# Moving the drains of woven matmul groups behind the next attention half step, in pieces

## Time and profile before

| what | us |
|---|---|
| median of 3 runs (1999.07 to 2000.43) | 1999.86 |
| the profiled execution's own time | 1998.55 |
| its span, first to last instruction | 1996.7 |
| PE busy in the span | 1897.4 (95%) |
| ACT busy | 906.2 (45%) |
| DVE busy | 778.3 (39%) |
| POOL busy | 661.8 (33%) |
| chain that ended last: share of PE | 82% |
| chain: DVE, ACT, issue | 9%, 6%, 3% |

### The profile page before, as it was taken

The page is one execution under the profiler, slowest core; times in us unless marked ns, Lnnn a source line. Parts: engine busy times, 40 slices in busy tenths (PEclk is TensorE's granted clock), DMA queues, the critical chain, the costliest instruction groups (busy, mean ns, idle before and its releaser), DMA issues.

```text
span 1996.7 us, 24926 instructions
## 1 busy us (share of the span) xinstructions
PE 1897.4 (95%) x9233; PEld 1546.8 (77%) x9239; DVE 778.3 (39%) x1346; ACT 906.2 (45%) x1775; POOL 661.8 (33%) x278
## 2 busy tenths in 40 slices
PE   8998999898999899989899999999999999999998
PEld 6887777676788777777676888888788878888886
DVE  3434655534543565544447672010350431111002
ACT  4555565543465556554353833233453353323222
POOL 2422333122242222322233444434103423444442
PEclk9998999999999899999999999999999999999999
DMA  4221212112322121211231222222102422222322
GB/s 153 85 74 43 74 65 74 53 43 106 116 85 66 51 72 66 74 53 43 104 138 65 95 95 95 86 94 89 60 1 75 142 78 97 95 95 95 99 101 85
DMA packets 44568, 163.74 MB, mean 82 GB/s; under 512 B 6192, under 2 KB 6448, under 8 KB 43824
## 3 DMA queue, kind: packets, MB, share of 16 engines
q1 hardware_dynamic: 42640, 148.65, 22.3%
q10 hardware_dynamic: 1824, 13.63, 1.8%
HBM read 155.97 MB, written 6.29 MB: 81 GB/s over the span
## 4 chain that ended last, share of the span: by engine, by line
PE 82%; DVE 9%; ACT 6%; issue 3%; DMA 0%; POOL 0%; DVEq 0%; ACTq 0%; POOLq 0%; SPq 0%
PE bank L644 12%; PE bank L646 12%; PE bank L645 12%; PE bank L647 10%; PE bank L649 10%; PE bank L648 10%; PE bank L771 2%; PE bank L788 2%; ACT q_dup L1013 2%; PE bank L749 1%; PE bank L747 1%; PE bank L750 1%; DVE y_tok L1398 1%; PE bank L735 1%; PE bank L708 1%
## 5 line engine op out<-in xcount | busy, mean ns | idle before, releaser
L627 POOL TENSOR_TENSOR w_hl<-w_raw,w_hl 128x1024 fp32r<-128x1024 f32 x274 | 661.6, 2419 | 1310.6 <-ACT w_hl L899 1310.0
L899 ACT ACTIVATE w_hl<-w_raw 128x1024 fp32r<-128x1024 f32 x274 | 287.6, 1058 | 343.7 <-DMA w_raw<-wstream 343.2
L644 PE MATMUL bank<-act_hl,w_hl 128*128 128x512 f32 x1056 | 428.4, 406 | 5.7 <-DVE q_low L1368 2.8
L646 PE MATMUL bank<-act_hl,w_hl 128*128 128x512 f32 x1056 | 415.4, 393 | 0.0
L645 PE MATMUL bank<-act_hl,w_hl 128*128 128x512 f32 x1056 | 415.1, 393 | 0.0
L647 PE MATMUL bank<-w_hl,act_hl 128*128 128x512 f32 x672 | 265.6, 395 | 6.1 <-DVE q_low L1368 4.0
L649 PE MATMUL bank<-w_hl,act_hl 128*128 128x512 f32 x672 | 262.3, 390 | 0.0
L648 PE MATMUL bank<-w_hl,act_hl 128*128 128x512 f32 x672 | 262.0, 390 | 0.0
L644 PEld LDWEIGHTS bank<-act_hl,w_hl 128*128 128x128 f32 x1056 | 201.1, 190 | 48.9 <-issue 5.7
L646 PEld LDWEIGHTS bank<-act_hl,w_hl 128*128 128x128 f32 x1056 | 200.2, 190 | 43.5
L645 PEld LDWEIGHTS bank<-act_hl,w_hl 128*128 128x128 f32 x1056 | 201.1, 190 | 40.3 <-issue 1.9
(11 more groups left out here) (232 smaller groups left out, 2839.7 us busy)
## 6 DMA issues: line engine op xcount, KB each, us to landing
w_raw<-wstream SPq DMA_DIRECT2D x274, 512.0 KB, 3.5
x_spill<-x_res ACTq DMA_DIRECT2D x2, 2048.0 KB, 7.0
x_res<-x_spill ACTq DMA_DIRECT2D x2, 2048.0 KB, 7.9
x_res<-x SPq DMA_DIRECT2D x4, 512.0 KB, 5.7
g_post<-post_gains ACTq DMA_DIRECT2D x4, 512.0 KB, 3.6
x_res<-x ACTq DMA_DIRECT2D x1, 2048.0 KB, 8.4
out<-x_res SPq DMA_DIRECT2D x4, 512.0 KB, 2.6
probs<-w_gates ACTq DMA_DIRECT2D x1, 1024.0 KB, 10.7
```

The costliest lines, as they stand in the source:

```text
L627: nc.gpsimd.tensor_tensor(w_hl[:, slot, 1].rearrange("p c n -> p (c n)"), w_raw[:, slot, :], w_hl[:, slot, 0].rearrange("p c n -> p (c n)" ...
L644: pe.matmul(out_ap, wh, ah, start=start, stop=False)
L646: return pe.matmul(out_ap, wl, ah, start=False, stop=stop)
L899: nc.scalar.activation(w_hl[:, b % RING, 0].rearrange("p c n -> p (c n)"), w_raw[:, b % RING, :], ACT.Copy).then_inc(s_high_done, 1)
```

## The change

- `weave` no longer puts a drain behind its block. It keeps drains in a list `pending`. After each attention half step one entry is taken from it. Before a half block with k == 0 (a group's first) all entries up to the last one that concerns its tiles are taken. What is left when the attention ends follows it.
- A drain step carries its tiles. A woven qk group has four pieces of one tile, an o group two pieces of two tiles, all others one piece of four. The pieces of tiles 0 and 1 hang on the last block's first half.
- The first segment beside sb and the first beside fox end at half step 12 instead of 15, and the first heads of fox stand at units 12 and 13 instead of 13 and 14, so that the fox gates end at half step 24 instead of 26.
- The recurrence keeps the old rule under the name `beside`.

```diff
-HEADS_AT = {"diff": (10, 13, 16, 18), "sb": (11, 12, 14, 17), "fox": (13, 14, 15, 17), "dil": (8, 13, 17, 18)}
+HEADS_AT = {"diff": (10, 13, 16, 18), "sb": (11, 12, 14, 17), "fox": (12, 13, 15, 17), "dil": (8, 13, 17, 18)}
@@ plan
-        out.append(("drain", len(groups) - 1))
+        out.append(("drain", len(groups) - 1, (0, 1, 2, 3)))
         return out
 
+    def halves(dense_steps):
+
+        out = []
+        for st in dense_steps:
+            if st[0] != "drain":
+                out += [(st[:4] + (tiles,), []) for tiles in ((0, 1), (2, 3))]
+                continue
+            tag = groups[st[1]]["tag"]
+            pieces = {"qk": [(0,), (1,), (2,), (3,)], "o": [(0, 1), (2, 3)]}.get(tag, [(0, 1, 2, 3)])
+            for tiles in pieces:
+                out[-1 if tiles[-1] > 1 else -2][1].append(st[:2] + (tiles,))
+        return out
+
     def weave(segments, others):
+
+
+        out, at, pending = [], 0, []
+        for dense_steps, upto in segments:
+            rest = halves(dense_steps)
+            n, seen = len(rest), 0
+            for i, other in enumerate(others[at:upto]):
+                while seen < math.ceil(n * (i + 1) / (upto - at)):
+                    block, drains = rest[seen]
+                    seen += 1
+                    while block[3] == 0 and any(set(st[2]) & set(block[4]) for st in pending):
+                        out.append(pending.pop(0))
+                    out.append(block)
+                    pending += drains
+                out.append(other)
+                if pending:
+                    out.append(pending.pop(0))
+            at = upto
+        return out + pending
+
+    def beside(segments, others):
@@
-                parts = [(output(l, 0) + project("qk", l, 1, 1), 15), (project("g", l, 1), done)]
+                parts = [(output(l, 0) + project("qk", l, 1, 1), 12), (project("g", l, 1), done)]
             else:
-                parts = [(project("qk", l, 2, 1), 15), (project("g", l, 2), done)]
+                parts = [(project("qk", l, 2, 1), 12), (project("g", l, 2), done)]
@@
-    steps += weave(parts + [(first_mix[:2], len(lru))], lru) + first_mix[2:]
+    steps += beside(parts + [(first_mix[:2], len(lru))], lru) + first_mix[2:]
@@
             g = groups[st[1]]
-            for j in range(4):
+            for j in st[2]:
                 take(("dense", st[1], j), j, signal=j < 3)
@@ scalar, vector
-            def drain(gi):
+            def drain(gi, tiles):
...
-                for j in range(4):
+                for j in tiles:
```

More of the change, by code:

```diff
@@ L539, in values_before @@
         for st in STEPS:
-            if st == ("drain", gi):
+            if st[:2] == ("drain", gi):
                 return n
@@ L1167, in _ @@
                 elif st[0] == "drain":
-                    drain(st[1])
+                    drain(st[1], st[2])
                     if st[1] + 1 in LAST:
@@ L1304, in forget, with drain @@
                 dve.wait_ge(s_ck_ready, l + 1)
-            def drain(gi, tiles=range(4)):
+            def drain(gi, tiles):
                 g = GROUPS[gi]
```

## The result

The changed kernel takes 2067.36 us, median of four runs (2062.54 to 2069.54), beside 1999.96 (1999.07 to 2000.43) for the kernel before: ratio 1.0334, 95% interval 1.0316 to 1.0353. It is slower, by 67 us. The forecast was 2055 with a range of 2024 to 2080.

What follows compares the result with a forecast made beforehand. PE, busy 1897.4 of 1996.7 us, was taken as the bound. Diff 7.4, sb 16.5, fox -0.7 and clock +4.3 made 27.5 a layer, 55 in both, on 1998.55: 2053.6, forecast as a median of 2055, range 2024 to 2080.

Steps and rivals of the forecast that it cites:

- Diff values and gates: Diff stage, drains behind half steps 18 and 8: banks free 4.4 and 4.2 us late, +3.7 each.
- First half of the sb queries and keys: Drained in four pieces over diff half steps 33 to 37: cost 0; at best it wins about 2.2 us.
- Output projection: First one in sb, tiles 2 and 3 behind half step 2: +2.5 us; the second projection costs nothing.
- Second half of the sb queries and keys: Sb half steps 10 to 12: waits of 1.7, 1.4 and 5.7 us, 8.8 instead of 1.6, so +7.2.
- Sb gates: Drain of the sb gates: PE idle 3.6 us instead of 0.62, so +3.0.
- First half of the fox queries and keys, fox values: Drained late in sb: queries and keys wait 5.0 us instead of 2.2, +2.5; fox values +1.3.
- Sb in sum: All sb terms together: +16.5 us a layer; sb should lengthen from 146 by 16 to 20.
- Second half of the fox queries and keys: Fox, in pieces: waits of 0.9 and 2.4 us, 3.3 instead of 6.5, so -3.2.
- Clock: Half-clock spells, per layer: the fox one goes, -2.5; four new idle stretches bring one each, +6.8; together +4.3 us.
- (a): Rival: same mechanism, PE idles more but no new half-clock spells come; 2041 us, chance 0.24.
- (b): Rival: many half-clock spells, seven a layer at 2.5 us; 2076 us, chance 0.13.
- (c): Rival: faster, as getting ACT's attention out ahead of the drain wins 29 us; 1970 us, chance 0.06.

Runs made afterwards that it cites:

- e1: The kernel before, with only the diff gates' drain moved behind half step 8 in each layer: 2006.12 us, ratio 1.0036.
- E3: e2 with only the queries and keys drained behind the half steps, in pieces: 2026.78 us, ratio 1.0143.
- e2: The changed kernel with every woven drain whole and ahead of the half step; only the moved segment ends and fox heads stay: 2010.89 us, ratio 1.0061.
- E7: The changed kernel with the segment ends and fox heads back at their old places, drains still in pieces and behind: 2048.62 us, ratio 1.0251.
- e9: The changed kernel with the sb gates started later, half steps 12 and 13 left without a block before them: 2052.02 us, ratio 1.0277.
- e8: The changed kernel with 48 added dummy matmuls a layer on PE during five bank waits of sb: 2050.39 us, ratio 1.0262.
- e5: The kernel before, with only the second half of the fox queries and keys drained in four pieces behind half steps 11 to 14: 1989.70 us, ratio 0.9954.
- e6: The changed kernel with every moved drain in one piece, behind the half step: 2071.97 us, ratio 1.0368.
- e10: e5 plus the changed kernel's fox heads at unit 12, with the gates' end kept at half step 26: 1980.75 us, ratio 0.9915.
- e12: e10 with the keys' pieces drained before the queries': 1988.38 us, ratio 0.9952.

## Why the prediction was right

The direction, the size within the range and the mechanism held: a drain behind the half step finds PE out of other work. By its own steps, first layer:

- **Diff values and gates** (4.4 and 4.2 of idle before the block): 4.11 and 4.08. PE's idle time in the stage grew by 7.6, forecast 7.4; the stage grew by 10.5, inside the 7 to 12. Right, and e1 shows the gates' term alone.
- **First half of the sb queries and keys** (0): the 1.64 for a bank went, and 1.70 for the turn of a head came. Right in sum, but by luck: the pieces delay attention there. E3, with the queries and keys behind, has the 1.7 too (1.68), e2, with all drains ahead, does not.
- **Output projection** (+2.5, and nothing for the second): 2.37 at the first, right. At the second PE waited 0.96, where I had nothing: a miss, small. It belongs to the moved end, as e2, with its drains ahead, has it too (0.97).
- **Second half of the sb queries and keys** (1.7, 1.4, 5.7): 1.59, 1.28, 5.43. Right; the waits of before there are 0.87 and 0.54, 1.4 instead of the 1.6 I took off. E7 and e9 show what the 5.43 hangs on: the half step that the new end puts between the two halves of the gates' block.
- **Sb gates** (3.6): 1.18 for the turn and 1.98 for the bank, 3.2.
- **First half of the fox queries and keys, fox values** (5.0 in three waits, and 1.3): 1.49 and 2.42, and 1.73. The third, of 0.6, didn't come: 3.9 and 1.7, each off by 0.4 to 1.1, in opposite directions.
- **Sb in sum**: idle time grew by 16.7, forecast 16.5. Its length grew by 24.2 (22.5 in the second layer) where I said 16 to 20: too small, since that figure had too little clock time in it. That the idle sum is so close is in part luck: the second output and the fox values came dearer, the fox queries and keys and the sb gates cheaper.
- **Second half of the fox queries and keys** (0.9 and 2.4 for 6.5): 0.85 and 2.40 for 6.51. Right. Fox changed by 3.1, the forecast was less than 3; its idle time fell by 2.7, where the terms gave 0.7, in part because turns in half steps without a block cost 7.9 and the gates 1.8, less than the 10.8 I had for them.
- **Clock** (+4.3 a layer, 8.6 in both): this is the term that was mis-sized. PE's busy time grew by 19.8. The prediction expected it "near 1900, more only by the half clock", and it is 1917.2. I let a spell follow each of four waits of over 3 us, at 1.7. All four came, in both layers, and five of the eight last 6.8 us instead of 3.4. What I had at nothing are spells behind shorter waits. In the two layers there are 18 spells, 81.9 us at the half clock, where before there were 8 with 41.0; the forecast made 14 of them. Two of the others, behind waits of 2.37 and 2.40:

```profile
232.08:235.48 3.40, 3.20 (x8) 2.53 (x9) 0.74 (x2) 0.00 (x0) 0.68 (x1) 0.50 0.00 0
433.46:436.88 3.42, 3.42 (x15) 2.93 (x13) 0.36 (x1) 0.49 (x1) 0.00 (x0) 0.50 0.12 20
```

  Spells stand behind the 2.42 in sb and the 1.80 of the fox gates too. In e8 five bank waits of sb are filled, none of 1.8 us or more is left there, and no spell comes.

In sum: idle time 44.2 of a forecast 46.4, clock 19.8 of 8.6, together 64.0 against 55.0. The other 3 us between 2055 and 2067 are that the runs of the changed kernel lie 5 above the profiled one, where I had added 1.3.

What I did not foresee is in e2: the earlier ends cost 11.6 by themselves, and 18.7 together with the moved drains (e7 against the change). I had priced them only through the drains and through fox's half steps without a block. The terms for sb came out right since each was worked out with the new end in it.

Of the rivals, (a) fell with the clock at 0.978 over the span. (b), with 17.5 less 2.5 a layer, was too much in us: the clock cost 9.9, between it and the forecast's 4.3. But its count was the better one: about seven new spells a layer came, as it had, only cheaper than its 2.5 each. (c), faster, fell for the change as a whole and is right for one group end: what it expected of the pieces came in e5, 0.46%. Elsewhere the pieces are worth little, 4.6 us over all of them (e6 against the change).

What stays open: which of the idle stretches bring the clock down. A spell began in or right behind each wait of 4.1 us in the changed kernel and in e1. Below that the same wait sometimes has one and sometimes not: the 3.42 in the first layer of e1 and not in its second, the 2.37 at the first output projection of the changed kernel and not the 2.35 at the same place of its second layer. E8 shows that the waits are what brings the spells, not what tells one from the other.

## What to carry to other kernels

Before a drain is moved behind other work, ask at each group end what the tensor engine still has to do between that work and the block which wants the bank; only in fox, where the whole drain stood ahead of attention and cost PE 6.5 us, and the pieces had half blocks and half steps between them, was there enough. Try each end alone: one of them was worth 0.5%, and 0.9% with the earlier heads, in a change that cost 3.3%. A wait can cost twice, once as idle time and again as time at half the clock, and here waits of about 2 us did so too, though not every time. A forecast that let only those over 3 us count had 8.6 of the 19.8 us.

## What the runs showed of the chip that I had not expected

- One moved wait of 4.1 us in a stretch of dense matmuls brought its own spell at half the clock (e1, 128.78 and 633.94) and yet left PE's busy time in the stage at 103.09 where it had been 103.08, and at 100.67 where it had been 102.81, since spells further on did not come. A stage's mean clock does not tell whether a wait was followed by a spell; the windows behind the wait do.
- Work that nobody needs made the kernel faster (e8): with the clock at 1.00 instead of 0.95 and 0.96, sb was 10.1 us shorter in the two layers together. The Trainium skill (TensorE: Matmul & The Clock Gate, "HAM oscillation — how this bites in real kernels") tells of a kernel whose clock falls in every wait for data, and counts half of the throttled time as loss. The half nearly agrees (matmuls 0.43 us apart against 0.23); that each wait brings a fall doesn't, by the 3.42 in the second layer of e1.
- The fall is not the same in the two layers of one execution: in sb of the changed kernel PE is idle for 21.1 us in both, and busy for 148.66 in the first, with four spells, and 147.15 in the second, with three. Nor is it the same in two runs of a program: four of the changed kernel spread by 7 us, at clocks of 0.975 to 0.978, and 17 of the kernel before, made beside e10 to e12, by 8.9 (1991.73 to 2000.59), at 0.988 to 0.991.
